# Shifting weight buffers by 8 to 32 bytes inside a 64-byte line

## The reference, cut to what matters

```
x = x + swiglu(rmsnorm(x), w_in, w_out)      # ffn0, hidden width 2816; ffn1, ffn2 and ffn3 alike
x = x + mlstm_mixer(rmsnorm(x))              # mixer 1
kv = compressed, selected and windowed keys and values of x
x = x + nsa_mixer(rmsnorm(x), kv)            # mixer 2
x = layer_norm(alpha * x + fox_mixer(x))     # mixer 3
x = layer_norm(alpha * x + dsa_mixer(x))     # mixer 4
swiglu(h, w_in, w_out): a, b = split(h @ w_in); return (silu(a) * b) @ w_out
```

## Time and profile before

| | us |
|---|---|
| median of 3 runs | 1311.35 (1310.18 to 1311.47) |
| span of the profiled execution | 1310.3 |
| TensorE busy in it | 1270.2 (97%) |
| VectorE busy | 873.9 (67%) |
| ScalarE busy | 613.6 (47%) |
| bytes moved by DMA | 218.17 MB, mean 167 GB/s |

### The profile page before, as it was taken

How to read it: one execution, slowest core, us unless ns; L and a number is a source line. 1 busy time by engine, 2 the same in 40 slices (tenths; PEclk the granted TensorE clock), 3 DMA queues, 4 the chain that set the end, 5 groups by cost and what they waited for, 6 DMA issues and landing times.

```text
span 1310.3 us, 16491 instructions
## 1 busy us (share of the span) xinstructions
PE 1270.2 (97%) x6717; PEld 1077.6 (82%) x6717; DVE 873.9 (67%) x1312; ACT 613.6 (47%) x839; POOL 24.2 (2%) x37
## 2 busy tenths in 40 slices
PE   6999999989999999999999999999999999999997
PEld 5888888988788888878888886778888899988876
DVE  6655557885755556685657569856555567566896
ACT  6444346435434445444435357654444344544461
POOL 2000000100000000000000000000000000000000
PEclk9999999999999999999999989999999999999999
DMA  9655545443555556565665440065666686446401
GB/s 329 207 182 187 186 162 185 142 155 129 183 184 185 188 192 186 166 193 170 217 224 169 159 161 1 1 200 187 191 193 193 130 217 172 150 130 211 176 2 65
DMA packets 158812, 218.17 MB, mean 167 GB/s; under 512 B 8257, under 2 KB 110993, under 8 KB 158737
## 3 DMA queue, kind: packets, MB, share of 16 engines
q1 hardware_dynamic: 156880, 212.56, 51.2%
q0 software_dynamic: 1376, 3.71, 0.9%
q10 hardware_dynamic: 480, 0.85, 0.2%
HBM read 216.04 MB, written 1.05 MB: 166 GB/s over the span
## 4 chain that ended last, share of the span: by engine, by line
PE 82%; DVE 11%; issue 3%; ACT 2%; SPq 1%; DMA 1%; DVEq 0%
PE PS L686 23%; PE PS L689 23%; PE PS L687 23%; DVE wlo L2050 2%; PE PS L823 1%; PE PS L721 1%; PE PS L722 1%; ACT whi L1523 1%; PE PS L706 1%; PE PS L1300 1%; DVE arena L2639 1%; PE PS L728 1%; PE PS L1016 1%; SPq L591 1%; DVE XL L2090 1%
## 5 line engine op out<-in xcount | busy, mean ns | idle before, releaser
L2050 DVE TENSOR_TENSOR wlo<-raw,whi 128x2048 fp32r<-128x2048 f32 (+4 forms) x206 | 457.4, 2230 | 122.6 <-ACT whi L1523 121.8
L1523 ACT ACTIVATE whi<-raw 128x2048 fp32r<-128x2048 f32 (+4 forms) x206 | 381.4, 1863 | 63.4 <-DMA raw<-in_fox_w_in_dram 33.1
L686 PE MATMUL PS<-whi,XL 128*128 128x512 f32 (+3 forms) x992 | 385.8, 390 | 8.9 <-DVE scr L2152 3.8
L687 PE MATMUL PS<-wlo,XH 128*128 128x512 f32 (+3 forms) x992 | 379.8, 384 | 0.0
L689 PE MATMUL PS<-whi,XH 128*128 128x512 f32 (+3 forms) x992 | 265.0, 384 | 0.0
L686 PEld LDWEIGHTS PS<-whi,XL 128*128 128x128 f32 x992 | 187.3, 189 | 45.1 <-DVE scr L2152 4.9
L689 PEld LDWEIGHTS PS<-whi,XH 128*128 128x128 f32 x992 | 185.5, 190 | 35.5
L687 PEld LDWEIGHTS PS<-wlo,XH 128*128 128x128 f32 x992 | 187.4, 189 | 32.9
L1577 ACT ACTIVATE scr<-PS,rn 128x256 f32<-128x256 f32 x88 | 41.7, 474 | 225.2 <-PE PS L689 223.9
L686 PE MATMUL PS<-whi,GL 128*128 128x512 f32 x320 | 125.4, 392 | 0.0
L687 PE MATMUL PS<-wlo,GH 128*128 128x512 f32 x320 | 124.6, 389 | 0.0
(11 more groups left out here) (387 smaller groups left out, 1339.2 us busy)
## 6 DMA issues: line engine op xcount, KB each, us to landing
raw<-in_ffn_w_in_dram SPq DMA_DIRECT2D x174, 512.0 KB, 5.0
raw<-in_ffn_w_out_dram SPq DMA_DIRECT2D x88, 512.0 KB, 4.9
raw<-in_fox_w_in_dram SPq DMA_DIRECT2D x24, 512.0 KB, 7.9
raw<-in_a_w_in_dram SPq DMA_DIRECT2D x16, 512.0 KB, 4.6
raw<-in_dsa_w_in_dram SPq DMA_DIRECT2D x16, 512.0 KB, 6.0
raw<-in_kv_w_dram SPq DMA_DIRECT2D x12, 512.0 KB, 4.2
raw<-in_fox_w_in_dram SPq DMA_DIRECT2D x12, 344.0 KB, 5.0
raw<-in_a_w_out_dram SPq DMA_DIRECT2D x8, 512.0 KB, 4.9
```

The costliest lines, as they stand in the source:

```text
L686: mm(o, xl, wh, start=start and i == 0, stop=False, skip_group_check=True)
L687: mm(o, xh, wl, start=False, stop=False, skip_group_check=True)
L1523: A(whi[:, p % SLOTS, 0:n], raw[:, p % SLOTS, 0:n], ACT.Copy).then_inc(hi_done, 1)
L2050: V.tensor_tensor(wlo[:, p % SLOTS, 0:n], raw[:, p % SLOTS, 0:n], whi[:, p % SLOTS, 0:n].bitcast(F32), ALU.subtract).then_inc(lo_done, 1)
```

## The change

A slot becomes 2056 numbers (8224 bytes, 128.5 lines), so that odd slots begin half a line off. `held(buf, p, n)` gives the place of piece p in its slot. A piece that is not named in `begins` still begins on a 64-byte boundary (offset 0 in even slots, 8 numbers in odd ones). The pieces of ffn1, ffn2 (those of the compression, loaded within it, too) and ffn3 begin 16, 8 and 24 bytes into a line in even slots, and as many bytes ahead of a boundary (48, 56 and 40 bytes in) in odd slots. The pieces of `B_CHUNK` chunks get 8, 16, 24 or 32 bytes by their place in the mixer, likewise mirrored in odd slots. A pad of 32 bytes after `whi` and another after `wlo` bring what follows back to a boundary, so `raw`, `whi` and `wlo` of a piece have the same offset in a line. ffn0, the A chunks and the output pieces of the mixers stay on boundaries.

The room comes out of `arena` (12672 to 12560 numbers): `n_gt` and the first part of `d_sel` move into `GL`'s memory, the rest of `d_sel` behind `d_wuv`, and some views inside `arena` move by 64 to 112 numbers, all multiples of 64 bytes. No instruction, wait or transfer is added or taken away.

```
+SLOT = PIECE + 8
...
+    begins = {}
+    for name, at in (("ffn1", 4), ("ffn2", 2), ("ffn3", 6)):
+        for p in range(first_piece[name], first_piece[order[order.index(name) + 1]]):
+            begins[p] = at
+    for name, (_, chunks) in stages.items():
+        p = first_piece[name]
+        for c, (kind, _, n) in enumerate(chunks):
+            for _ in range(2 if n * KT > PIECE else 1):
+                if kind == B_CHUNK:
+                    begins[p] = 2 * (c % 4) + 2
+                p += 1
...
-        whi = sb("whi", [P, SLOTS, PIECE], F32R)
+        whi = sb("whi", [P, SLOTS, SLOT], F32R)
+        sb("half_line", [P, 8])
...
-        wlo = sb("wlo", [P, SLOTS, PIECE], F32R)
-        raw = nc.alloc_sbuf_tensor_at("raw", [P, SLOTS, PIECE], F32, offset=lo_at)
+        wlo = sb("wlo", [P, SLOTS, SLOT], F32R)
+        raw = nc.alloc_sbuf_tensor_at("raw", [P, SLOTS, SLOT], F32, offset=lo_at)
+
+        def held(buf, p, n=PIECE):
+
+            at = begins.get(p, 0)
+            at = 8 - at if p % SLOTS % 2 else at
+            return buf[:, p % SLOTS, at:at + n]
+
+        sb("half_line_2", [P, 8])
...
-                        dst = raw[:, p % SLOTS, :].rearrange("p (k w n) -> p k w n", k=4, w=2)
+                        dst = held(raw, p).rearrange("p (k w n) -> p k w n", k=4, w=2)
...
-                return (whi[:, p % SLOTS, :].rearrange("p (k n) -> p k n", k=k),
-                        wlo[:, p % SLOTS, :].rearrange("p (k n) -> p k n", k=k))
+                return (held(whi, p).rearrange("p (k n) -> p k n", k=k),
+                        held(wlo, p).rearrange("p (k n) -> p k n", k=k))
...
-                A(whi[:, p % SLOTS, 0:n], raw[:, p % SLOTS, 0:n], ACT.Copy).then_inc(hi_done, 1)
+                A(held(whi, p, n), held(raw, p, n), ACT.Copy).then_inc(hi_done, 1)
...
-                V.tensor_tensor(wlo[:, p % SLOTS, 0:n], raw[:, p % SLOTS, 0:n], whi[:, p % SLOTS, 0:n].bitcast(F32),
+                V.tensor_tensor(held(wlo, p, n), held(raw, p, n), held(whi, p, n).bitcast(F32),
                                 ALU.subtract).then_inc(lo_done, 1)
```

More of the change, by code:

```diff
@@ L166, in program @@
         d_work = nc.alloc_sbuf_tensor_at("d_work", [P, 384], F32, offset=gl_at)
+        d_sel0 = nc.alloc_sbuf_tensor_at("d_sel0", [P, P], F32, offset=gl_at + 4 * 384)
+        n_gates = nc.alloc_sbuf_tensor_at("n_gates", [P, 96], F32, offset=gl_at)
         GHz = nc.alloc_sbuf_tensor_at("GHz", [P, 2, T], F32R, offset=xs_at + 4 * D)
@@ L188, in program @@
         n_cm = sb("n_cm", [P, 3 * 32])
-        AW = 12672
+        AW = 12560
         arena_at = (nc.sbuf_base + 31) // 32 * 32
@@ L260, in program @@
         t_PT = t_PT.rearrange("p (b s j t) -> p b s j t", b=2, s=2, j=4)
-        n_qT, n_gt, n_cs, n_cpT = carve(keep, 2048, 96, 1024, 1024)
+        n_qT, n_cs, n_cpT = carve(keep, 2048, 1024, 1024)
         n_qT = n_qT.rearrange("p (k t) -> p k t", k=KT)
-        n_gt = n_gt.rearrange("p (t c) -> p t c", t=NT)
+        n_gt = n_gates[:, :].rearrange("p (t c) -> p t c", t=NT)
         n_cs = n_cs.rearrange("p (t h n) -> p t h n", t=NT, h=QH)
         n_cpT = n_cpT.rearrange("p (t g q) -> p t g q", t=NT, g=KVH)
-        f_qT, f_kT, f_v, f_gate, d_sel = carve(0, 2048, 2048, 2048, 2048, 384)
+        f_qT, f_kT, f_v, _, f_gate = carve(0, 2048, 2048, 2048, 64, 2048)
         f_qT = f_qT.rearrange("p (k t) -> p k t", k=KT)
@@ L279, in program @@
         d_kT = d_kT.rearrange("p (k t) -> p k t", k=KT)
-        d_ckr, d_ckvT, d_krT, d_wuv = carve(4096, 320, 256, 256, 1024)
+        d_ckr, d_ckvT, d_krT, d_wuv, d_sel1 = carve(4096, 320, 256, 256, 1024, 256)
         d_ckr = d_ckr.rearrange("p (t c) -> p t c", t=NT)
@@ L570, in _ @@
                         k = src.shape[1]
-                        dst = raw[:, p % SLOTS, 0:n].rearrange("p (k n) -> p k n", k=k)
+                        dst = held(raw, p, n).rearrange("p (k n) -> p k n", k=k)
                         for part in (slice(0, k // 2), slice(k // 2, k)):
@@ L596, in load_out @@
                     free_slot(p)
-                    dst = raw[:, p % SLOTS, :].rearrange("p (k n) -> p k n", k=2)
+                    dst = held(raw, p).rearrange("p (k n) -> p k n", k=2)
                     for w in range(2):
@@ L605, in load_cmp @@
                         free_slot(p)
-                        dst = raw[:, p % SLOTS, :].rearrange("p (k n) -> p k n", k=8)
+                        dst = held(raw, p).rearrange("p (k n) -> p k n", k=8)
                         src = rows(a["cmp_w1"][kv], 8 * half, 8, 0, 256)
@@ L913, in parts_n @@
             def parts_n(p, k, n):
-                return (whi[:, p % SLOTS, 0:k * n].rearrange("p (k n) -> p k n", k=k),
-                        wlo[:, p % SLOTS, 0:k * n].rearrange("p (k n) -> p k n", k=k))
+                return (held(whi, p, k * n).rearrange("p (k n) -> p k n", k=k),
+                        held(wlo, p, k * n).rearrange("p (k n) -> p k n", k=k))
             def out_part(name, t, i):
@@ L2881, in choose @@
                 cols = slice(0, P) if t == 0 else slice(P, 384)
-                work, isc, sel_ = d_work[:, cols], d_isc[:, cols], d_sel[:, cols]
+                work, isc, sel_ = d_work[:, cols], d_isc[:, cols], d_sel0[:, :] if t == 0 else d_sel1
                 cm = caus[:, P:2 * P] if t == 0 else caus
@@ L2916, in d_mask @@
             def d_mask(t, g, j):
-                return d_sel[:, 0:P] if t == 0 else d_sel[:, P:384]
+                return d_sel0[:, :] if t == 0 else d_sel1
             split_to(first + 12)
```

## The result

The changed kernel takes 1328.88 us (median of 4; 1327.97 to 1330.95) against 1311.41 (median of 4; 1310.18 to 1314.27) in the same comparison: ratio 1.0131, interval 1.0114 to 1.0148, +17.5 us. A second comparison gave 1328.78 us and 1.0126 (1.0101 to 1.0150). The direction was as predicted; the size was not: 1316.0 was forecast, and 1328.9 lies above the range.

The account below looks back on a forecast made before the run. TensorE was taken as the bound, through the distance between matmul starts, everywhere but in dsa's middle. 1310.3 + 7.1 (moving weights) - 2.5 (held weights) = 1314.9 us, plus 1.05 from span to median: 1316.0; range 1298 to 1327.

Parts of the forecast that it names:

- Moving weights off a boundary: ffn1, ffn2, ffn3: 2376 matmuls dearer by 3.0 ns each, +7.1 us; ends -7.8 and +14.7 us.
- (c): Unsettled 512-column matmuls after a break in ffn1: 232.9 ns each, 6.2 ns more than settled ones.
- (a): dsa's 372-column moving rows beginning at 0, 16, 32 and 48 bytes: 170.6 ns each, 2.3 above the steady extra.
- (b): fox's 344-column moving rows beginning at 0 and 32 bytes: 157.0 ns each, 0.4 above the steady extra.
- the yardstick: ffn0 and the mixers' output products: expected to keep 226.6 ns per start, as reference for the changed blocks.
- Held weights: Eight B chunks off dsa, 768 matmuls: 3.3 ns less each, -2.5 us; other end +1.8 us.
- Copies, landing, moved buffers: Copies into `whi` and `wlo`, landing of loads and buffers moved by whole lines: costed at nothing.
- Faster: Rival: any offset between two operands lowers the extra; 10.3 us less, 1301 us; chance 0.29.
- rows 7: Timeline of ffn2's compression: held activations 32 bytes into a line, aligned moving weights, 46 starts 116.7 ns each.
- (d): ffn2's compression, held activations 32 bytes into a line: 116.7 ns each, 3.3 less; used to price held weights.
- Re-settles: Rival of no real change: matmuls settle at 13.3 ns extra again, paying only at slot changes; about 1311.7; chance 0.18.
- One line more: Rival: moving rows starting inside a line always read one line more, 2376 x 6.7 = +15.8 us; about 1326; chance 0.11.

Follow-up runs that it names:

- even_128: Against the kernel before: all weights moved by 128 bytes relative to the held activations, slots 8192 bytes apart; 1328.04 us, ratio 1.0110.
- stride_only: The changed kernel with all pieces beginning on a 64-byte line again, the longer slots kept; 1323.96 us, ratio 1.0081 to the kernel before.
- moved_buffers: The change's buffer moves kept, but slots 8192 bytes apart and beginning where they did modulo 256 bytes; 1311.70 us, ratio 0.9994 to the kernel before.
- even_16: Against the kernel before: all weights moved by 16 bytes relative to the held activations, slots 8192 bytes apart; 1324.35 us, ratio 1.0092.
- held_128: Against the kernel before: weights left in place, held activations and all behind them moved by 128 bytes; 1330.37 us, ratio 1.0142.
- the scan: Slots 8192 bytes apart, weight pieces' begin falling lap by lap from 252 to 4 bytes behind the held activations modulo 256; 1333.56 us, one execution.

## Why the prediction was wrong

*What bounds the kernel.* Right: the loss lies in the distance between TensorE's starts, and no wait was added.

*Moving weights off a boundary, 2376 x 3.0 = +7.1 us.* This step failed, first in its size. The distance rose by 232.8 - 227.4 = 5.4 ns, and 2376 x 5.4 = +12.8 us. Of the three rows averaged, only (c), the unsettled 512-column matmuls, had such a price, 232.9 ns. But those were in step, and no run shows that being unsettled and being out of step cost the same for the same reason, so its nearness may be luck. (a) and (b) could not show the price: even_128 moves those rows by 128 bytes and leaves them where they were (170.6 and 170.4 ns, 157.3 and 157.1), while rows of 384 numbers, six times 256 bytes, go from 173.7 to 176.0. Rows of 372 and 344 numbers are no multiple of 256 bytes long; in the kernel before one row in four is in step, and it costs hardly less than the other three (169.7 against 170.8 ns, 157.2 against 157.4). Why these widths show no price stays open. The settled 13.3 ns from which I measured them are what 512 columns pay in step.

*"ffn0 and the mixers' output products keep their 226.6 ns and are the yardstick."* This step failed outright. I looked at where a piece begins inside its line and not at the slot's length, which went from 8192 to 8224 bytes for every piece. The 1608 matmuls of 512 columns that "stay on a line" rose by 231.2 - 227.4 = 3.8 ns: +6.1 us that stood in no term. stride_only, with nothing but that left, is 0.8% slower than before.

*Held weights, 768 x -3.3 = -2.5 us.* The sign was right, the size a third: 119.3 against 120.6 ns, 768 x -1.3 = -1.0 us, because offsets and slot lengths spread the pieces over many places. At 8 bytes alone the gain is there, 2.2 us in fox's six chunks.

*Copies, landing, moved buffers: nothing.* Right: 2290 and 1911 ns, no new wait, and moved_buffers at 0.9994. Not counted was the compression, whose moving weights lie in ffn2: 96 x (120.7 - 116.6) = +0.4 us. The sum with the sizes found is 12.8 + 6.1 - 1.0 + 0.4 = +18.3 us; +17.5 was measured. That this is so near is in part luck. The two profiled spans differ by 18.9 us; without the 4.8 us in the nsa part that no distance explains, and the 2.0 us by which the start was shorter, 16.1 are left. The sum takes every matmul as setting the end, and how many of the mixers' do not, no run here shows.

*The rivals.* "Faster" had rows 7 for it, an operand 32 bytes out. The place of one operand against the other was the right quantity, as (d) considered, but the sign of those 256-column matmuls does not carry over: none of the places scanned has a 512-column mean below the one in step. (The single short distance of rows 7, 113 ns in the trace, is 7 below 120.0 and not 6, and is one step of a cycle from 113 to 120.) "Re-settles" fails as the main course: in even_16, even_128 and held_128 no out-of-step stretch comes back to 226.7. The steady stretch at 112 bytes in the scan shows that it can happen. "One line more" came nearest in time, but for a wrong reason: a row that begins two lines further on, as in even_128, reads no line more and pays all the same. The 16-byte lines of the Trainium skill, "SBUF — State Buffer", section "Specifications (TRN2)", would have given nothing for even_16 and even_128, which cost 0.92% and 1.10% (10 and 14 us by the medians); the measurement decides.

Still open is what inside the chip counts in 256 bytes, why 112 bytes has two levels, and why 4 bytes ahead is free while 4 bytes behind is the dearest place (237.8 ns). No run here looks below the distance between starts.

## What to carry to other kernels

Before pricing a shifted operand, write down the place of both operands of each matmul, and of the next one's held operand, modulo the distance that a run has shown to matter (256 bytes here), for every slot of the ring: padding that changes a slot's length shifts all pieces, also those that the edit leaves "aligned". A reference row must show that it reacts to the shift before a price is read from it: the 344- and 372-column rows here do not. And a step that was to stay fixed, the yardstick, deserves the same look as the steps that change.

## What the hardware showed that I had not expected

With 512 columns the distance settled at 226.7 ns wherever the moving rows, the held operand and the next held operand lay at the same place modulo 256 bytes. Out of step its mean is 229 to 238 ns, in short cycles, with two exceptions: 4 bytes ahead (227.4, seen in one run) and single stretches at 112 bytes (226.7). With 256 columns being out of step can pay: held weights go from 120 ns in step to 115.6 at 8 bytes. Not everywhere, though: the compression, out of step in both kernels, goes from 116.6 to 120.7.
